# One layer's conditioning product computed in plain float32 on column lanes

## The reference, cut to what matters

```python
def adaln(cond, ada_w, ada_b):
    m = jax.nn.silu(cond) @ ada_w + ada_b          # [1024] @ [1024, 3072]
    return jnp.split(m, 3, axis=-1)

def modulate(x, gain, shift, scale):
    return rms_norm(x, gain) * (1 + scale) + shift

# in both layers, for the latent tokens (c) and for the context tokens (c_ctx)
shift, scale, gate = adaln(c, ada_w, ada_b)
shift_c, scale_c, gate_c = adaln(c_ctx, ada_w, ada_b)
u = modulate(x, norm_g, shift[:, None], scale[:, None]) @ w_in
uc = modulate(ctx, norm_g, shift_c, scale_c) @ w_in
```

## Time and profile before

| what | value |
|---|---|
| median of 3 runs | 3406.09 us (3399.55 to 3413.08) |
| profiled execution | 3406.72 us, span 3404.9 us |
| PE busy | 3028.6 us, 89% |
| DVE busy | 1541.5 us, 45% |
| ACT busy | 1084.7 us, 32% |
| mean granted PE clock | 0.909 of full |

### The profile page before, as it was taken

How to read it: one execution, slowest core, us unless ns; L and a number is a source line. 1 busy time by engine, 2 the same in 40 slices (tenths; PEclk the granted TensorE clock), 3 DMA queues, 4 the chain that set the end, 5 groups by cost and what they waited for, 6 DMA issues and landing times. The chain is left out here.

```text
span 3404.9 us, 54059 instructions
## 1 busy us (share of the span) xinstructions
PE 3028.6 (89%) x23282; PEld 2340.5 (69%) x23282; DVE 1541.5 (45%) x2580; ACT 1084.7 (32%) x1965; POOL 34.6 (1%) x52
## 2 busy tenths in 40 slices
PE   7799889989878888887899999698887999999998
PEld 3488656877747888446788777456566777778876
DVE  5523346353463444655454324354444344455522
ACT  5411357232242322212322222463223232332222
POOL 0000000000001111000000000000000000000000
PEclk9899999999969999798899999678887799989998
DMA  8511100123031111201233222301220122223321
GB/s 272 142 56 56 35 1 19 45 87 118 20 140 61 41 40 28 95 1 50 87 93 95 87 81 68 91 1 57 56 77 2 32 81 86 75 68 95 93 89 64
DMA packets 232560, 236.99 MB, mean 70 GB/s; under 512 B 28040, under 2 KB 205704, under 8 KB 232257
## 3 DMA queue, kind: packets, MB, share of 16 engines
q1 hardware_dynamic: 232018, 232.35, 22.4%
q10 hardware_dynamic: 304, 1.18, 0.1%
HBM read 213.89 MB, written 19.09 MB: 68 GB/s over the span
## 5 line engine op out<-in xcount | busy, mean ns | idle before, releaser
L201 DVE TENSOR_TENSOR second_w_low<-second_w_raw,second_w_high 128x1024 fp32r<-128x1024 f32 (+1 forms) x228 | 272.6, 1197 | 535.2 <-ACT second_w_high L197 535.1
L197 ACT CAST second_w_high<-second_w_raw 128x1024 fp32r<-128x1024 f32 (+1 forms) x228 | 232.9, 1023 | 664.1 <-PE ffn_in_acc L222 256.5
L220 PE MATMUL ffn_in_acc<-ffn_h_high,second_w_high 128*128 128x512 f32 x704 | 282.7, 402 | 14.2 <-DVE ffn_h_low L578 14.2
L222 PE MATMUL ffn_in_acc<-ffn_h_high,second_w_low 128*128 128x512 f32 x704 | 284.4, 404 | 0.0
L221 PE MATMUL ffn_in_acc<-ffn_h_low,second_w_high 128*128 128x512 f32 x704 | 281.1, 399 | 0.0
L201 DVE TENSOR_TENSOR first_w_low<-first_w_raw,first_w_high 128x1024 fp32r<-128x1024 f32 x115 | 140.2, 1223 | 263.8 <-ACT first_w_high L197 263.1
L197 ACT CAST first_w_high<-first_w_raw 128x1024 fp32r<-128x1024 f32 x115 | 120.1, 1047 | 229.9 <-PE attn_in_acc L222 80.1
L220 PEld LDWEIGHTS ffn_in_acc<-ffn_h_high,second_w_high 128*128 128x128 f32 x704 | 134.4, 191 | 48.8 <-issue 17.8
L221 PEld LDWEIGHTS ffn_in_acc<-ffn_h_low,second_w_high 128*128 128x128 f32 x704 | 134.5, 191 | 34.4 <-issue 0.5
L220 PE MATMUL attn_in_acc<-attn_h_high,first_w_high 128*128 128x256 f32 (+1 forms) x416 | 143.8, 346 | 14.4 <-DVE attn_h_low L323 14.4
L222 PEld LDWEIGHTS ffn_in_acc<-ffn_h_high,second_w_low 128*128 128x128 f32 x704 | 134.4, 191 | 31.3
(11 more groups left out here) (755 smaller groups left out, 6514.8 us busy)
## 6 DMA issues: line engine op xcount, KB each, us to landing
second_w_raw<-in_ffn_w_gate SPq DMA_DIRECT2D x44, 512.0 KB, 3.8
second_w_raw<-in_ffn_w_up SPq DMA_DIRECT2D x44, 512.0 KB, 3.8
second_w_raw<-in_ffn_w_down SPq DMA_DIRECT2D x40, 512.0 KB, 3.4
first_w_raw<-in_rec_w_in SPq DMA_DIRECT2D x33, 512.0 KB, 3.9
first_w_raw<-in_attn_ada_w SPq DMA_DIRECT2D x24, 512.0 KB, 4.8
first_w_raw<-in_rec_ada_w SPq DMA_DIRECT2D x24, 512.0 KB, 4.8
second_w_raw<-in_w_in SPq DMA_DIRECT2D x24, 512.0 KB, 3.9
second_w_raw<-in_w_branch_gate SPq DMA_DIRECT2D x24, 512.0 KB, 3.6
```

Source lines behind the costliest of these rows:

```text
L197: act.copy(self.view(self.high[b % self.splits], b), self.view(self.raw[b % self.bufs], b)).then_inc(self.high_done, 1)
L201: dve.tensor_tensor(self.view(self.low[b % self.splits], b), self.view(self.raw[b % self.bufs], b), self.view(self.high[b % self.splits], ...
L220: pe.matmul(out, sh, mh, start=(first and j == 0), stop=False)
L222: ins = pe.matmul(out, sl, mh, start=False, stop=(last and j == len(parts) - 1))
```

## The change

The three products of a split become one plain float32 product that reads the raw block, so ACT and DVE no longer split the 48 conditioning blocks; PE itself raises `w_split_done` when it has used a block. The stationary operand is padded from 2 to 32 columns, and feature tile k goes to lane k % 4: PSUM partitions 32 x lane to 32 x lane + 31. Four lanes therefore hold four partial sums of each result, in 128 rows, and `adaln_rows` has 128 partitions. The turn no longer transposes: it multiplies the 128 x 128 piece with a matrix `pick` of 128 x 2 that has ones where the four lanes hold the same row, which adds the lanes up. Blocks 48 and 49 are split after block 47, not between the others.

```diff
@@ class WeightStream
+        self.whole = 0 if whole is None else self.ranges[whole][1]
...
     def make_low(self, dve, b):
-        dve.wait_ge(self.high_done, b + 1)
+        dve.wait_ge(self.high_done, b + 1 - self.whole)
...
+LANES, LANE = 4, 32
+def lane_rows(nc, name, w, x, evict, aside):
+    b0, b1 = w.ranges[name]
+    per = KD // len(w.blocks[b0][2])
+    following = range(b1, w.split_limit(name))
...
+        @block.tensor
+        def _(pe):
+            for b in range(b0, b1):
+                ks, n = w.blocks[b][2], (b - b0) // per
+                pe.wait_ge(w.landed[b % w.bufs], w.landings[b])
+                if n >= slots and ks[0] == 0:
+                    pe.wait_ge(stored[n % 2], (n - slots) // 2 + 1)
+                raw = w.view(w.raw[b % w.bufs], b)
+                for j, k in enumerate(ks):
+                    lane = k % LANES
+                    ins = pe.matmul(ps[n % slots][lane * LANE:lane * LANE + LANE, :], x(k), raw[:, j, :],
+                                    start=(k < LANES), stop=(k >= KD - LANES), skip_group_check=True)
+                ins.then_inc(w.split_done, 1)
+                aside.pe(pe, b - b0)
...
+        @block.vector
+        def _(dve):
+            for b in range(b0, b1):
+                evictions(dve, 0, b)
+                aside.dve(dve, b - b0)
+            dve.wait_ge(w.split_done, b1)
+            for b in following:
+                w.make_low(dve, b)
+        @block.scalar
+        def _(act):
+            for b in range(b0, b1):
+                evictions(act, 1, b)
+                aside.act(act, b - b0)
+            for b in following:
+                w.make_high(act, b, b1, None, None)
 def adaln(nc, w, cond, layers, ident, aside):
-        rows = keep.enter_context(nc.sbuf_tensor("adaln_rows", [2, len(layers) * 3 * D], F32))
-        high, low = (keep.enter_context(nc.sbuf_tensor("adaln_cond_" + n, [P, KD, 2], F32R)) for n in ("high", "low"))
+        rows = keep.enter_context(nc.sbuf_tensor("adaln_rows", [P, len(layers) * 3 * D], F32))
+        silu = keep.enter_context(nc.sbuf_tensor("adaln_silu", [P, KD, LANE], F32))
+        pick = keep.enter_context(nc.sbuf_tensor("adaln_pick", [P, 2], F32))
...
-        linear_tokens(nc, "adaln", w, lambda k: high[:, k, :], lambda k: low[:, k, :], 2,
-                      lambda e, g, t, ps: copy_on(e, nc, rows[:, BANK * g:BANK * g + BANK], ps[0:2, :]), aside=aside)
+                dve.memset(silu[:], 0.0).then_inc(cleared, 1)
+                chain.link(dve.tensor_tensor(pick[:], ident[:, 0:2], ident[:, LANE:LANE + 2], ALU.add))
+                for lane in range(2, LANES):
+                    chain.link(dve.tensor_tensor(pick[:], pick[:], ident[:, LANE * lane:LANE * lane + 2], ALU.add))
+        lane_rows(nc, "adaln", w, lambda k: silu[:, k, :],
+                  lambda e, g, ps: copy_on(e, nc, rows[:, BANK * g:BANK * g + BANK], ps[:]), aside)
...
-                        ins = pe.transpose(ps[:, i, n, :], rows[:, at:at + P], ident[0:2, 0:2])
+                        ins = pe.matmul(ps[:, i, n, :], rows[:, at:at + P], pick[:], start=True, stop=True)
```

More of the change, by code:

```diff
@@ L124, with __init__ @@
 class WeightStream:
-    def __init__(self, nc, stack, name, blocks, bufs=4, splits=3):
+    def __init__(self, nc, stack, name, blocks, bufs=4, splits=3, whole=None):
         def sb(n, dtype):
@@ L807, in _, with evictions @@
                     low_part(pool, k)
+LANES, LANE = 4, 32
[3 more added lines that the diff above has]
+    following = range(b1, w.split_limit(name))
+    with Stage(nc, name) as st:
+        slots = 4
+        ps = [st.ps(f"acc{i}", [P, BANK]) for i in range(slots)]
+        stored = (st.sem("stored_v"), st.sem("stored_a"))
+        aside.begin(st)
+        block = st.block()
+        @block.sync
+        def _(sp):
+            w.load_stage(sp, name)
+        @block.tensor
[12 more added lines that the diff above has]
+                aside.pe(pe, b - b0)
+        def evictions(engine, which, b):
+            n = (b - b0) // per
+            if w.blocks[b][2][-1] == KD - 1 and n % 2 == which:
+                engine.wait_ge(w.split_done, b + 1)
+                evict(engine, n, ps[n % slots]).then_inc(stored[which], 1)
+        @block.vector
[13 more added lines that the diff above has]
+                w.make_high(act, b, b1, None, None)
@@ L815, in adaln @@
         with Stage(nc, "adaln_silu") as st:
-            silu = st.sb("silu", [P, KD, 2])
-            silu_done, high_done = st.sem("silu_done"), st.sem("high_done")
+            cleared, own = st.sem("cleared"), st.sem("own")
             block = st.block()
@@ L821, in _ @@
             def _(act):
-                act.activation(silu[:], cond, ACT.Silu).then_inc(silu_done, 1)
-                act.wait_ge(silu_done, 1)
-                act.copy(high[:], silu[:]).then_inc(high_done, 1)
+                act.wait_ge(cleared, 1)
+                act.activation(silu[:, :, 0:2], cond, ACT.Silu)
             @block.vector
             def _(dve):
-                dve.wait_ge(high_done, 1)
-                dve.tensor_tensor(low[:], silu[:], high[:].bitcast(F32), ALU.subtract)
-        linear_tokens(nc, "adaln", w, lambda k: high[:, k, :], lambda k: low[:, k, :], 2,
-                      lambda e, g, t, ps: copy_on(e, nc, rows[:, BANK * g:BANK * g + BANK], ps[0:2, :]), aside=aside)
+                chain = Chain(dve, own)
+                dve.memset(silu[:], 0.0).then_inc(cleared, 1)
[4 more added lines that the diff above has]
+                  lambda e, g, ps: copy_on(e, nc, rows[:, BANK * g:BANK * g + BANK], ps[:]), aside)
         with Stage(nc, "adaln_turn") as st:
@@ L3969, in program @@
                 "adaln": [b for n in ("attn", "rec") for b in weight_blocks(d[n + "_ada_w"], 0, 3 * D, width=512)],
-                **attn_weights(d), **rec_weights(d)})
+                **attn_weights(d), **rec_weights(d)}, whole="adaln")
             load(nc, "vectors", [(vec[:], d["vec"]), (const[:], d["c_small"])])
```

## The result

The kernel after takes 3425.04 us (median of 6 runs, 3417.93 to 3429.27), the kernel before on the same chip 3402.95 (6 runs, 3399.55 to 3413.08). The ratio is 1.0049, with a 95% interval of 1.0035 to 1.0064: slower by half a per cent, with a ratio of 1 outside the interval. The forecast was 3414, in a range of 3402 to 3426.

What follows compares the result with a forecast made beforehand. It took the stage as PE-bound in blocks 8 to 15, then bound by the buffers' round trip; -7.5 us there and +15.7 in the turn gave +8.2 on 3406.7, predicted 3414 us, range 3402 to 3426.

Steps and rivals of the forecast that it cites:

- The first part: Start to the end of block 7, queued behind `x` and `ctx`: done at about 31 us, before about 33.
- A block on PE: Four passes of a conditioning block, two at a time: 0.86 us of PE, 1.65 us from landing to release.
- a rival: All lanes at once: 0.43 us of PE per block, stage ends at 99.4, 3407 us; chance 0.08.
- Blocks 8 to 15: PE-bound stretch with root sums: steps of 2.16 us instead of 2.64, PE at 48.3 us instead of 54.1.
- sixteen changes of mode: Tiling mode changes around the root sums that drain the engine: estimated 2.6 us on the sum, 3417 instead of 3414.
- Blocks 16 to 47: Stretch bound by the buffer round trip: 6.55 us a round, 1.64 per block, 52.5 us, ending at 100.8.
- loads that don't follow: Rival: a shorter round only slows landings, blocks 16 to 47 still take 1.77 us each; 3418 us, chance 0.13.
- The tail: Blocks 48 and 49, split after block 47: 5.6 us where it was 3.1, stage ends at 106.4 instead of 113.9.
- The turn: After the product stage: 96 plain float32 passes at half clock, 0.217 each, 20.8 us, 15.7 more than before.
- the +8.2 of the sum: Net forecast change: 7.5 us gained by the product stage, 15.7 lost in the turn.
- the series case: Rival: lanes don't overlap, steps of 3.02 us in blocks 8 to 15, stage ends at 117.3; 3425 us, chance 0.08.
- The rival of a clock that falls in the product stage: PE's clock halves while waiting for landings: steps of 4.3 us, stage ends at 133.9; 3441 us, chance 0.06.

Runs made afterwards that it cites:

- roots_apart: Kernel after with a group of root sums behind every second block instead of behind each of blocks 8 to 15; 3412.91 us, ratio 1.0024 to the kernel before.
- turn_plain: Kernel before with the 48 transposes of the turn written as plain float32 products with the same two-row stationary; 3425.24 us, ratio 1.0055.
- warm_turn: Kernel after with seven useless products of 512 columns ahead of the turn; 3427.8 us, ratio 1.0067 to the kernel before.
- few_sums: Kernel after without five of the six root products in each group from the second on; 3409.6 us, ratio 1.0007 to the kernel before.
- sums_only: Kernel after with DVE adding the squares and one group of root products replacing eight; 3409.27 us, ratio 1.0001 to the kernel before.
- one_lane: Kernel after with all eight feature tiles in one lane of 32 partitions; 3429.77 us, ratio 1.0066 to the kernel before.
- roots_thin: Kernel after with two of a group's six root products behind each of blocks 8 to 31; 3418.8 us, ratio 1.0033 to the kernel before.
- thin_add: Kernel after with two root products behind each of blocks 8 to 31, lanes added by DVE, and transposes in the turn; 3399.1 us, ratio 0.9984 to before.
- sums_add: Kernel after with DVE adding squares (one root group for eight) and lanes, and transposes in the turn; 3386.8 us, ratio 0.9949 to the kernel before.

## Why the prediction was right in its range and wrong in a step

Two numbers of each term, forecast and measured, all on the profiled executions:

- **The first part.** Block 7 done at 31; block 8 starts at 29.62. 1.4 us better.
- **A block on PE.** Two lanes at a time, 0.86 us. Nearly right for a block by itself: it has 0.98 of a step in the root stretch and takes 1.05 with its tail, where one lane alone took 1.8 (3.27 less the root sums). The order was another one: the four passes start in two pairs 0.45 us apart, so both lanes end together, 0.4 us sooner than 2 x 0.43 + 0.59. And where two landed blocks stand side by side, four lanes run at once, for 0.45 us a block at full clock (roots_apart) and 0.85 at half (blocks 16 to 19 of the kernel after). The forecast had left that to a rival because a block holds only two lanes; it came true wherever PE had two blocks in hand.
- **Blocks 8 to 15.** Steps of 2.16 us, 17.3 in all; measured 30.5 us (29.62 to 60.09), 13.2 more. This is the step that failed. At full clock the steps were 2.42 to 2.60, so about 0.3 of each was mis-sized: 8 x 0.3 = 2.4 us. That is the size of the 2.6 us that the forecast named for sixteen changes of mode and left out of its sum, though no run separates such a change from a longer root group. The other 11 are the granted clock, 0.50 from 36.4 to 63.7 us.
- **Blocks 16 to 47.** 52.5 us forecast; 51.4 measured (60.09 to 111.45), of it 1.64 per block from block 20 on (66.03 to 110.40), as forecast, with a longer landing (5.4 for 4.9) and a shorter way from landing to release. The forecast had named a landing of 5.4 as the mark of loads that don't follow; they followed all the same, and the 1.64 came out right by two errors that cancel.
- **The tail.** 5.6 us; 5.9 measured (111.45 to 117.38). SP needed 10.85 us for the sixteen pieces where I took 9.63.
- **The turn.** 20.8 us at half clock; 20.61 measured. The choice of the 0.217 row over the 0.116 of the earlier trace rows was worth 10 us and was right. turn_plain shows 96 records of 0.21 us, and warm_turn a clock that this turn doesn't keep even with wide products ahead of it. Most of the loss is in this term, and the forecast had it.

Together -1.4 + 13.2 - 1.1 + 0.3 - 0.2 = 10.8 us above the +8.2 of the sum, 19.0 in all; the trace shows 18.9. By the prediction's own test ("wrong if that instruction is not between 2 us earlier and 14 us later") it was wrong. That 3425 still lies inside the range of 3402 to 3426 is luck: the upper end was set to take in most of the series case, which is not what happened.

The rival of a clock that falls in the product stage was the right mechanism with the wrong reason and size. It was argued from PE's waits for landings and dismissed because four passes in 1.64 us keep PE about as busy. In the profiled execution that held: from block 20 on the clock is 1.00 in spite of the waits (30.68 of 48 us busy), and it fell where PE doesn't wait. In other runs of the lanes it did fall in stretches of waits: twice in few_sums, three times in warm_turn, once each in roots_apart (100.5) and sums_only, each time behind a wait of 1.3 to 2.1 us and for 3.4 us only, and by no means behind every such wait. With root sums among the blocks of the lanes the long fall of each run lasts 20 to 65 us. The earlier trace rows had the hint: PE busy 19.94 of 20 us with PEld at 12.04, against 5.77 in the next window, says that this stretch is made of many short products; the change cut the wide ones from 1.39 to 0.98 us a step and left every short one. The price of 3441 assumed half clock to the end of the stage, and it lasted 27 us. The series rival reached the measured 3425 by another way: its steps were 3.02 us at full clock and the clock was to stay up; one_lane, which is that case, took 3.27 a step. That its number was hit is chance.

The Trainium skill (TensorE: Matmul & The Clock Gate, HAM oscillation) puts a clock that falls down to waits between bursts of matmuls, DMA waits above all. The short falls in few_sums and warm_turn stand behind such waits, but the trace of the kernel after doesn't bear that out as the only way: before the fall PE is busy 7.88 us of 8, and at half clock 10.00 of 10.

```profile
28.00:36.00 8.00, 7.88 (x46) 0.90 0.94 317
38.00:48.00 10.00, 10.00 (x36) 0.50 0.47 149
```

(Windows of the kernel after, PE alone; the 0.90 holds the last of the half clock that the wait for `x` and `ctx` had left.) The fourfold gain of TensorEngine Tiling (Array Packing), Theoretical Speedup, also of the Trainium skill, agrees with the trace where two landed blocks stand side by side: eight passes take 1.06 us at full clock in roots_apart, and two blocks in one lane took twice 1.8. A block by itself, with two lanes, shows a twofold gain, and the round trip of the loads gives PE mostly such blocks.

Shown is that root sums between the blocks of the lanes bring the long slow phase, since sums_only has one group in place of eight, computes the same, and has no such phase. Why they do stays open: the runs give two mixtures that keep the clock (before, one_lane) and three that don't (after, roots_apart, roots_thin), not a rule.

## What to carry to other kernels

Making the wide products cheaper changes the mixture in which small ones stand. Before lanes or another packing shorten a stretch, count the small products that remain on TensorE beside them, here the root sums, and move them to an idle engine first; here the same edit was worth 1.4 us before the lanes and 16 after. And price a plain float32 product used as a transpose at four times the transpose: twice the records, and 0.213 us instead of 0.107 for each at the same half clock. Adding on VectorE ahead of it made the turn 15 us cheaper than letting the product add.

## What the hardware showed that I had not expected

- The granted clock fell from 1.00 to 0.50 with PE busy 7.88 of the 8 us up to 36.0, and stayed there for 27.3 us without a gap in its work (in thin_add for 64.9).
- The same four passes that take 1.05 us by themselves take 1.06 us together with four of the next block, when both have landed: four column lanes run side by side.
- Transposes of 2 x 128 take 0.107 us each at half clock, plain float32 products of the same operands 0.427 (two records).
- A turn of 96 plain float32 records takes 19.83 us with 2 rows in the stationary, 20.61 with 32 and 20.61 with 128.
- Fillers of 512 columns held the clock up for 2 us of the turn and saved 1.8 of its 20.6 us.
- VectorE adds two rows of 512 in 0.69 us, as long as it takes to copy 128 rows of 512 (0.69 us in the kernel after): sums_add has 44 such steps from 20 to 100 us, 30 us of VectorE, beside the loads.
